# Moving the rotary-angle chain on GpSimd from the gate stage to the first FFN part

## What is computed

```python
# first block
merged = sigmoid(ga) * (attn @ w_attn_branch) + sigmoid(gc) * (conv @ w_conv_branch)
h = h + merged @ w_out
hn = rms_norm(h, ffn_norm)
up = causal_depthwise_conv(hn @ w_up, ffn_conv_w)        # 1024 -> 2 * 2816, three taps
gate, val = split(up, 2)
h = h + (silu(gate) * val) @ w_down
# second block, once for both layers
ang = positions[:, None] * inv_freq[None, :]
cos, sin = cos(ang), sin(ang)                            # used by apply_rotary on q and k of retention
```

## Time and profile before

| what | value |
|---|---|
| time, median of three | 1233.79 us |
| profiled execution: time, span | 1233.25 us, 1231.4 us |
| mean granted clock of TensorE | 0.995 |
| PE busy | 1216.4 us, 99% |
| DVE, ACT, POOL busy | 841.0, 589.7, 283.9 us |
| gate stage | about 132 to 265 us |
| rotary chain on POOL | about 136 to 246 us |
| first FFN part, up / down products | about 309 to 397 / 397 to 440 us |

### The profile page before, as it was taken

The page is one execution under the profiler, slowest core; times in us unless marked ns, Lnnn a source line. Parts: engine busy times, 40 slices in busy tenths (PEclk is TensorE's granted clock), DMA queues, the critical chain, the costliest instruction groups (busy, mean ns, idle before and its releaser), DMA issues.

```text
span 1231.4 us, 15972 instructions
## 1 busy us (share of the span) xinstructions
PE 1216.4 (99%) x6095; PEld 1033.1 (84%) x6095; DVE 841.0 (68%) x1373; ACT 589.7 (48%) x1076; POOL 283.9 (23%) x299
## 2 busy tenths in 40 slices
PE   8999999999999999999999999999999999999998
PEld 7888888888888888888887879899888889899886
DVE  6799665556777357744768787767747776776756
ACT  6666332333444224423437377754435477655442
POOL 0220599902000000000006561111313211111310
PEclk9999999999999999999999899999999999999999
DMA  8422333333433333333224243222214332222211
GB/s 229 125 69 69 95 103 99 89 103 97 126 100 89 103 98 90 103 95 94 86 69 137 63 114 89 78 71 71 82 52 138 95 103 87 77 69 69 73 49 69
DMA packets 196033, 114.37 MB, mean 93 GB/s; under 512 B 3994, under 2 KB 190836, under 8 KB 195828
## 3 DMA queue, kind: packets, MB, share of 16 engines
q1 hardware_dynamic: 195956, 113.35, 31.6%
HBM read 111.23 MB, written 2.10 MB: 92 GB/s over the span
## 4 chain that ended last, share of the span: by engine, by line
PE 93%; DVE 2%; issue 2%; ACT 1%; POOL 1%; DMA 1%; SPq 0%; DVEq 0%; POOLq 0%; ACTq 0%
PE ps L180 91%; PE ps L183 3%; POOL sums L160 1%; DVE b_sets L160 1%; DMA xtm<-in_x_dram 1%; ACT whi L157 0%; DVE wlo L160 0%; ACT b_p L157 0%; DVE b_pt L160 0%; DVE b_s L163 0%; SPq L186 0%; DVE b_sets L163 0%; ACT x0h L157 0%; ACT sums L157 0%; DVE tmp L160 0%
## 5 line engine op out<-in xcount | busy, mean ns | idle before, releaser
L157 ACT ACTIVATE whi<-raw 128x1024 fp32r<-128x1024 f32 (+1 forms) x198 | 206.3, 1050 | 312.1 <-PE ps L180 311.8
L160 DVE TENSOR_TENSOR wlo<-raw,whi 128x1024 fp32r<-128x1024 f32 (+1 forms) x192 | 244.4, 1279 | 50.0 <-ACT whi L157 49.0
L180 PE MATMUL ps<-x0h,whi 128*128 128x512 f32 x1008 | 256.9, 393 | 0.6 <-ACT x0h L157 0.6
L180 PE MATMUL ps<-x0l,whi 128*128 128x512 f32 x1008 | 257.1, 393 | 0.3 <-DVE x0l L163 0.3
L180 PE MATMUL ps<-x0h,wlo 128*128 128x512 f32 x1008 | 254.2, 390 | 0.0
L180 PEld LDWEIGHTS ps<-x0h,whi 128*128 128x128 f32 x1008 | 188.7, 189 | 39.3 <-ACT x0h L157 1.0
L180 PEld LDWEIGHTS ps<-x0h,wlo 128*128 128x128 f32 x1008 | 187.6, 188 | 38.1
L180 PEld LDWEIGHTS ps<-x0l,whi 128*128 128x128 f32 x1008 | 186.5, 188 | 38.2 <-DVE x0l L163 0.6
L160 POOL TENSOR_TENSOR sums<-sums,sq 128x512 f32<-128x512 f32 x28 | 42.0, 1510 | 429.9 <-ACT sq L157 429.9
L180 PE MATMUL ps<-x1h,wlo 128*128 128x512 f32 x304 | 82.3, 389 | 0.0
L180 PE MATMUL ps<-x1h,whi 128*128 128x512 f32 x304 | 82.3, 389 | 0.0
(11 more groups left out here) (177 smaller groups left out, 1713.1 us busy)
## 6 DMA issues: line engine op xcount, KB each, us to landing
raw<-in_w_in_dram SPq DMA_DIRECT2D x98, 512.0 KB, 4.0
raw<-in_w_up_dram SPq DMA_DIRECT2D x44, 512.0 KB, 3.8
raw<-in_w_out_dram SPq DMA_DIRECT2D x24, 512.0 KB, 3.7
raw<-in_w_down_dram SPq DMA_DIRECT2D x16, 512.0 KB, 3.8
b_m<-in_rel_bias_dram SPq DMA_DIRECT2D x16, 256.0 KB, 3.4
raw<-in_w_down_dram SPq DMA_DIRECT2D x8, 384.0 KB, 3.4
xtm<-in_x_dram SPq DMA_DIRECT2D x4, 512.0 KB, 6.7
raw<-in_w_attn_branch_dram SPq DMA_DIRECT2D x8, 256.0 KB, 2.9
```

Source lines behind the costliest of these rows:

```text
L157: return AC.put(lambda e: e.activation(o, i, func, **kw), after, AC, 1)
L160: return on.put(lambda e: e.tensor_tensor(o, a, b, op), after, on, 1)
L180: return PE.put(lambda e: e.matmul(o, l, r, start=start, stop=stop), after, PE if mark else None, 1)
```

## The change

The chain is emitted later: no longer ahead of the gate stage but behind the first two up tiles of the first FFN part. Its scratch is a region of its own, `RT`, at the end of the FFN layout, in place of `DEC`, `ROT`, `TMP` and `RX`, which goes. As `RT` overlaps what the gate stage reads, the load of the positions waits for `h_tok[7]`, the last output tile of `w_out`. The load of `DEC` is emitted just behind the load of the positions and waits for nothing. The sines read `RT` and write `ROT`.

```diff
-        RX = at("rx", 512, (pool_off + 4 * (4096 * 2 + 1024 + 2048 + 514 * 2 + 512 * 2 + 384) + 31) // 32 * 32)
-        _, UB, CB = pool_plan("f_", [("sums", 2048, F32), ("u", 4 * 514, F32), ("c", 4 * 512, F32)])
+        _, UB, CB, RT = pool_plan("f_", [
+            ("sums", 2048, F32), ("u", 4 * 514, F32), ("c", 4 * 512, F32), ("rt", 8 * 512, F32)])
...
-        rot = {}
-
-        def rotary_turns():
-            R_ = [DEC[:, 0:512], DEC[:, 512:1024], DEC[:, 1024:1536], ROT[:, 512:1024],
-                  DEC[:, 1536:2048], TMP[:, 2560:3072], RX[:, :], ROT[:, 0:512]]
...
-            t_pos = dma(R_[0].bitcast(I32), bass.AP(tensor=positions_2.tensor, offset=positions_2.offset,
-                                                     ap=[[0, 128], [1, 512]]), d_pos)
...
-        rotary_turns()
-
         ths = Slots([ZC[:, 512 * i:512 * i + 512] for i in range(4)])
...
+        rot = {}
+
+        def rotary_turns():
+            R_ = [RT[:, 512 * i:512 * i + 512] for i in range(8)]
+            p = lambda o, a, s1, s2, op0, op1=None, after=(): ts(o, a, s1, s2, op0, op1, after=after, on=PO)
+            b = lambda o, a, c, op, after=(): tt(o, a, c, op, after=after, on=PO)
+            free = h_tok[7]
+            t_pos = dma(R_[0].bitcast(I32), bass.AP(tensor=positions_2.tensor, offset=positions_2.offset,
+                                                     ap=[[0, 128], [1, 512]]), d_pos, after=free)
...
+            for a, n in ((R_[1], 5), (R_[2], 4)):
+                for i in range(n):
+                    t = p(R_[4], a, TURN[i], None, ALU.mult, after=t)
+                    t = copy(R_[5].bitcast(I32), R_[4], after=t, on=PO)
+                    t = copy(R_[6], R_[5].bitcast(I32), after=t, on=PO)
+                    t = b(R_[4], R_[4], R_[6], ALU.subtract, after=t)
+                    t = b(R_[3], R_[3], R_[4], ALU.add, after=t)
+                    t = whole(R_[3], t)
+            t = p(R_[7], R_[3], 0.25, None, ALU.add, after=t)
+            rot["turns"] = whole(R_[7], t)
+            rot["dec"] = dma(DEC[:, :], const_d, d_dec)
+
+        def rotary_sines():
+            c = act(ROT[:, 0:512], RT[:, 7 * 512:8 * 512], ACT.Sin, scale=TWOPI, after=[rot["turns"], t_c])
+            rot["tok"] = [c, act(ROT[:, 512:1024], RT[:, 3 * 512:4 * 512], ACT.Sin, scale=SGN, after=rot["turns"])]
+
         for pi, (a, b) in enumerate(PARTS):
...
                 first_tiles(evs[:2], norm_steps(1e-5)[1])
                 evs = evs[2:]
-                rot["dec"] = dma(DEC[:, :], const_d, d_dec, after=rot["turns"])
+                rotary_turns()
```

More of the change, by code:

```diff
@@ L840, in block_then_hybrid_layers @@
                 proj(ev(j))
-        rot = {}
-        def rotary_turns():
-            R_ = [DEC[:, 0:512], DEC[:, 512:1024], DEC[:, 1024:1536], ROT[:, 512:1024],
-                  DEC[:, 1536:2048], TMP[:, 2560:3072], RX[:, :], ROT[:, 0:512]]
-            p = lambda o, a, s1, s2, op0, op1=None, after=(): ts(o, a, s1, s2, op0, op1, after=after, on=PO)
-            b = lambda o, a, c, op, after=(): tt(o, a, c, op, after=after, on=PO)
-            t_pos = dma(R_[0].bitcast(I32), bass.AP(tensor=positions_2.tensor, offset=positions_2.offset,
-                                                     ap=[[0, 128], [1, 512]]), d_pos)
[L851 to L877, removed]
-        rotary_turns()
         ths = Slots([ZC[:, 512 * i:512 * i + 512] for i in range(4)])
@@ L1026, in evac_up, with whole @@
             return go
+        rot = {}
[6 more added lines that the diff above has]
+                                                     ap=[[0, 128], [1, 512]]), d_pos, after=free)
+            t = copy(R_[1], R_[0].bitcast(I32), after=t_pos, on=PO)
+            t = p(R_[0], R_[1], INVF, None, ALU.mult, after=[t, t_c])
+            t = p(R_[1], R_[0], 4097.0, None, ALU.mult, after=t)
+            t = b(R_[2], R_[1], R_[0], ALU.subtract, after=t)
+            t = b(R_[1], R_[1], R_[2], ALU.subtract, after=t)
+            t = b(R_[2], R_[0], R_[1], ALU.subtract, after=t)
+            t = memset(R_[3], 0.0, after=t)
+            magic = 12582912.0
+            def whole(dst, tok):
+                tok = p(R_[6], dst, magic, -magic, ALU.add, ALU.add, after=tok)
+                return b(dst, dst, R_[6], ALU.subtract, after=tok)
+            for a, n in ((R_[1], 5), (R_[2], 4)):
[12 more added lines that the diff above has]
+            rot["tok"] = [c, act(ROT[:, 512:1024], RT[:, 3 * 512:4 * 512], ACT.Sin, scale=SGN, after=rot["turns"])]
         for pi, (a, b) in enumerate(PARTS):
```

## The result

The changed kernel takes 1242.76 us (median of four runs, 1240.86 to 1242.97) against 1234.34 us: ratio 1.0065, 95% interval 1.0048 to 1.0083. It is 8.4 us slower; 6 us were forecast. Three more executions of it took 1239.80, 1243.84 and 1244.65 us. One execution of one later kernel, the first with idle matmuls, ran at a granted clock of 0.75 from end to end (1516.23 us) and is left out of that kernel's median.

A forecast was written before the change was run, and what follows sets the result against it. PE, busy 99% of the span, was taken as the bound. DVE's lateness beyond its room, with lost clock, gave 5.8 to 7.2 us; 6 on 1233.25 made 1239.3, plus 0.5 for the median 1239.8; range 1233.4 to 1248.

The forecast's parts named there:

- Gate stage: gain 0: Gate stage: taking the chain's 73 POOL instructions and the positions DMA away gains 0, as PE had no wait there.
- the rival in which POOL's traffic slows PE: Gate stage: without POOL's traffic PE gains 1.6 us, 2.5 with a miscount: 1231.3 us, chance 0.05.
- The port and its times: SBUF reads: POOL and DVE take turns; POOL holds 1.15 us with two inputs, 0.46 with one; DVE 0.56 to 1.10.
- One check of it: Six `b_sets` of DVE beside POOL: port times give 3.35 us per POOL pair and three DVE instructions, 1.12 each.
- The walk: 12.04 us per pair: FFN part 0, turn by turn: a gate and value tile take DVE 12.04 us against PE's 10.88, falling back 1.16.
- the bounds of 0.4 and 3.2: FFN part 0: lower and upper estimates, in us, of how far DVE falls back per pair of tiles.
- The start: 5.7 us late: FFN part 0, from 324.2: the chain's opening and 14 contending DVE instructions bring `f_u` of 336.99 to 342.7.
- What is late for PE: Part 0's down products: sixth-index `x1l` 12.0 us late, room 8.3, PE stands 3.8; last about 14 late, 5.8 in all.
- The clock: Behind PE's stop in part 0's down products: clock at 1.2 GHz for most of 10 us, costing 3.4 us.
- two sums: Part 0's down products: first stop plus low clock, 3.8 + 3.4 = 7.2 us, or the last tile's lateness, 5.8 us.
- The 6 us: Whole kernel: extra time taken from a range of 5.8 to 7.2 us, giving a median of 1239.8 us.
- Loads, `DEC`, sines: FFN: weight loads delayed 0.58 us under cover, `DEC` first read a layer later, sines after the chain: nothing lost.

The follow-up runs named there:

- memset run: Changed kernel with each of the nine rounds of the chain replaced by fifteen 128x512 POOL memsets, angles left out: 1234.23 us, ratio 1.0001.
- one-input run: Changed kernel with the three two-input POOL instructions of each round replaced by one-input ones: 1234.50 us, ratio 1.0003.

## Why the prediction was right, point by point

*Gate stage: gain 0.* Right. PE's busy time and its 132 or 133 matmuls in 30 us are as before, without POOL; the rival in which POOL's traffic slows PE is out.

*The port and its times.* Right, shown by the two runs that change only what POOL runs in its rounds. One check of it was a little off: the six `b_sets` of the earlier trace rows are all tensor_tensor, so a POOL pair and three of them make 1.15 + 0.46 + 3 x 0.56 = 3.29 us, 1.10 each and not 1.12; 1.11 were measured. On the Trainium skill's page "SBUF — State Buffer", section "Who interferes with whom": that a GpSimd instruction which only writes doesn't exclude DVE's two-input instruction agrees with the memset run (749 ns). The page calls the shared ports an exclusive lock, and writes of a hold for the whole instruction where it speaks of DVE's 2-port modes. For two SBUF inputs of DVE this doesn't agree here when POOL's instruction has one input (0.45 of 1.50 us, and a loss of nothing in the one-input run).

*The walk: 12.04 us per pair.* This is the term that was mis-sized. From 343.27 to 406.29 five pairs took 63.0 us, 12.6 each; the first two took 13.15 and 13.18, the last 11.8. The walk had DVE always ready. The trace shows it idle for about 0.16 us before `x1l` and before the stt from `tmp`, waiting for ACT's half, and that shifts the turns. The walk had casts beside the value tile's two stt. In the first three pairs the trace has two-input instructions there (1.15 us of port time against 0.46), and the two stt take 2.79 to 3.47 us. In the last two pairs it has one-input instructions, the two stt take 1.88 (403.77), and the pairs, 12.1 and 11.8 us, are those of the walk. The fall per pair was 1.7 us on average for 1.16, inside the bounds of 0.4 and 3.2. What shifts the turns was read from the trace and not tried by itself.

*The start: 5.7 us late.* It was 5.0, with a chain that began at 327.13, or 325.9 with the 1.26 us taken off, and not at 324.2. With the walk this gives 5.0 + 5 x 1.72 = 13.6 us at tile 15, for 11.5.

*What is late for PE.* Right in place and order: the sixth feature first. Its `x1l` was 14.1 us late (done at 408.06) for a forecast of 12.0, with the room of 8.3. PE stood for 5.0 us, waiting for `x1h`, for 3.8. The last feature's `x1l`, done at 419.82, was 15.7 us late for about 14, so it alone would hold PE back by 7.4 us for 5.8.

*The clock.* 3.4 us, as forecast. The forecast had two sums, the stop plus the clock and the last feature's lateness, of which the larger holds: 7.2 and 5.8 us. The trace bears this out: 5.0 + 3.4 = 8.4 against the 7.4 that the last feature forces. Both were larger than forecast because of the walk.

*The 6 us.* By its own sums the forecast should have been 7.2 us, about 1241.0, and the 6 that it took, near the lower of the two, has no reason behind it. So of the 2.4 us that are missing, about half is this choice and half the stop, 5.0 for 3.8.

*Loads, `DEC`, sines.* Nothing, as forecast; the first is shown by its run, the others show no new wait of PE in the trace.

## What to carry to other kernels

Work on an idle engine isn't free when it reads through a port that a busy one needs, unless the delay stays within what the busy engine has left, as it did with one-input instructions: before moving POOL work, count DVE's instructions with two SBUF inputs in the stage it goes to, and take turn by turn what they wait. A queue that falls back by 10 to 20% per tile costs nothing until its lateness is more than the room ahead of some reader, and then costs all the rest; so a long chain belongs where DVE is half idle or ends a few tiles ahead of the due time. When PE must wait, look at which need comes next before paying for its clock.

## What the runs showed of the hardware

A 128x512 stt of DVE on SBUF took 749 ns beside a POOL that only wrote (91% busy), 952 ns beside one-input and 1221 ns beside mixed one- and two-input instructions. A POOL that read with one input did so at 95% busy and cost nothing end to end (ratio 1.0003). PE's clock stayed at 2.4 GHz after stops of 1.33 and 0.30 us amid wide matmuls in the one profiled execution of that kernel (three of its other six were some 3 us longer at a lower mean clock), and fell to 1.2 GHz after one of 4.97 us, and also after gaps of 0.57, 0.28 and 0.47 us followed by sixteen matmuls one column wide; with those gaps filled it stayed up, narrow matmuls and all.
